# Second block's projection: value columns multiplied 512 at a time from a ring of four weight places, outputs stored by whole token tiles

## What is computed

```python
h = jnp.concatenate([meta, x], axis=1)             # 1040 x 1024
p = rms_norm_2(h, norm_mix_pre[l]) @ w_in[l]       # w_in: 1024 x 3080
pa = p[..., :A_COLS]                               # 512 columns, recurrent unit
pb = p[..., A_COLS:A_COLS + B_COLS]                # 512 q, 512 k, 512 v, 8 forget gates
pc = p[..., A_COLS + B_COLS:]                      # 1024 columns, delta rule
```

## Time and profile before

| | |
|---|---|
| median of 3 runs | 3685.35 us (3679.71 to 3690.36) |
| profiled execution, span first to last instruction | 3696.6 us |
| mean granted TensorE clock | 0.951 of full speed |
| PE busy | 3382.9 us, 92% of the span |
| DVE, ACT, POOL busy | 44%, 33%, 7% |
| DMA | 289.30 MB, mean 78 GB/s |
| the phase of the second projection | about 1825 to 2194.6 us of the span |
| its value part | 2099.1 to 2191.7 us |

### The profile page before, as it was taken

How to read it: one execution, slowest core, us unless ns; L and a number is a source line. 1 busy time by engine, 2 the same in 40 slices (tenths; PEclk the granted TensorE clock), 3 DMA queues, 4 the chain that set the end, 5 groups by cost and what they waited for, 6 DMA issues and landing times. The chain is left out here.

```text
span 3696.6 us, 52585 instructions
## 1 busy us (share of the span) xinstructions
PE 3382.9 (92%) x21754; PEld 2898.5 (78%) x21754; DVE 1628.7 (44%) x2517; ACT 1222.9 (33%) x2230; POOL 260.5 (7%) x332
## 2 busy tenths in 40 slices
PE   7899978999798999897999999887888899999998
PEld 2699976777587999775788985556666799999777
DVE  2306725666472111365444104554554455554343
ACT  3212315666562343125442103443322211111232
POOL 2000000000010000112201100001210000000010
PEclk9999998999899999998999996998999899999999
DMA  9224550000342221334211220001003111111332
GB/s 329 88 84 149 159 175 36 12 12 13 132 156 98 76 74 58 110 115 139 92 34 48 86 71 12 13 3 5 2 2 115 63 45 45 45 46 56 108 128 93
DMA packets 196721, 289.30 MB, mean 78 GB/s; under 512 B 41606, under 2 KB 137670, under 8 KB 194480
## 3 DMA queue, kind: packets, MB, share of 16 engines
q1 hardware_dynamic: 176624, 216.90, 18.0%
q0 software_dynamic: 19904, 69.65, 5.7%
HBM read 217.60 MB, written 68.90 MB: 78 GB/s over the span
## 5 line engine op out<-in xcount | busy, mean ns | idle before, releaser
L115 PE MATMUL p_pb<-p_w_hi,h_hi 128*128 128x416 f32 (+2 forms) x1216 | 425.1, 350 | 7.8 <-DVE p_w_lo L110 7.8
L117 PE MATMUL p_pb<-p_w_hi,h_lo 128*128 128x416 f32 (+2 forms) x1216 | 422.3, 347 | 0.0
L116 PE MATMUL p_pb<-p_w_lo,h_hi 128*128 128x416 f32 (+2 forms) x1216 | 420.0, 345 | 0.0
L115 PE MATMUL fu_pf<-h_hi,fu_w_hi 128*128 128x344 f32 (+1 forms) x1056 | 339.4, 321 | 8.6 <-DVE fu_pf L3439 8.6
L116 PE MATMUL fu_pf<-h_lo,fu_w_hi 128*128 128x344 f32 (+1 forms) x1056 | 340.3, 322 | 0.0
L117 PE MATMUL fu_pf<-h_hi,fu_w_lo 128*128 128x344 f32 (+1 forms) x1056 | 338.9, 321 | 0.0
L115 PEld LDWEIGHTS p_pb<-p_w_hi,h_hi 128*128 128x128 f32 x1216 | 229.4, 189 | 16.9 <-issue 15.5
L116 PEld LDWEIGHTS p_pb<-p_w_lo,h_hi 128*128 128x128 f32 x1216 | 229.5, 189 | 1.9
L117 PEld LDWEIGHTS p_pb<-p_w_hi,h_lo 128*128 128x128 f32 x1216 | 229.1, 188 | 0.7
L115 PEld LDWEIGHTS fu_pf<-h_hi,fu_w_hi 128*128 128x128 f32 x1056 | 199.9, 189 | 9.0 <-DVE fu_pf L3439 9.0
L117 PEld LDWEIGHTS fu_pf<-h_hi,fu_w_lo 128*128 128x128 f32 x1056 | 199.8, 189 | 0.0
(11 more groups left out here) (521 smaller groups left out, 7188.6 us busy)
## 6 DMA issues: line engine op xcount, KB each, us to landing
mod_w<-in_adaln_w SPq DMA_DIRECT2D x12, 2048.0 KB, 16.8
fu_raw<-in_ffn_up SPq DMA_DIRECT2D x88, 256.0 KB, 3.1
fd_raw<-in_ffn_down SPq DMA_DIRECT2D x44, 512.0 KB, 3.6
la_qkv<-p SPq DMA_DIRECT2D x16, 1024.0 KB, 4.9
p<-p_o SPq DMA_DIRECT2D x60, 208.0 KB, 1.9
s_raw<-in_w_in POOLq DMA_DIRECT2D x48, 256.0 KB, 3.5
rT<-p_stage SPq DMA_DIRECT2D x10, 896.0 KB, 4.8
p_raw<-in_ab_w_in POOLq DMA_DIRECT2D x10, 832.0 KB, 6.2
```

The costliest lines, as they stand in the source:

```text
L115: pe.matmul(out, left[0], right[0], start=start, stop=False)
L116: pe.matmul(out, left[0], right[1], start=False, stop=False)
L117: return pe.matmul(out, left[1], right[0], start=False, stop=stop)
```

## The change

A class `WeightRing` takes the place of `Weights` in this phase: one pair `w` of `[128, 8, 512]` with four places of 128 columns side by side; block `b` is made at place `b % 4`. The raw buffer is as before (one, in halves). The last four blocks, the value columns, fill all four places, and the value uses read 512 columns across them. A value use is now one token tile: 9 uses (21 to 29) of 24 matmuls with 512 moving columns, in place of 12 uses of 72 matmuls with 128. Since all value blocks must be in place before the first value use, the table `prepared_at` makes two blocks at the starts of blocks 17 and 18, one at 19, and the last one (23) at the start of use 21; that one overwrites block 19, which use 20 reads. The copy of a use is one of 128 x 512 (16 x 512 for the first) into the first 512 columns of the q/k output buffer `x`, and the store one of whole 2 KB rows. The buffers `vo` go.

```diff
...
+class WeightRing:
+    def __init__(self, ph, kd, blk, n):
+        self.half, self.blk, self.n = kd // 2, blk, n
+        self.raw = [ph.sb(f"raw{h}", [P, self.half, blk]) for h in range(2)]
+        self.w = ph.pair("w", [P, kd, n * blk])
+        self.raw_in = ph.sems("raw_in0 raw_in1")
+        self.hi_done = ph.sems("hi_done0 hi_done1")
+        self.lo_done = ph.sems("lo_done0 lo_done1")
+    def part(self, b, h, which):
+        c0 = self.blk * (b % self.n)
+        return self.w[which][:, self.half * h:self.half * h + self.half, c0:c0 + self.blk]
+    def load(self, eng, b, src):
+        for h in range(2):
+            if b:
+                eng.wait_ge(self.lo_done[h], b)
+            eng.dma_start(self.raw[h][:, :, :], src(self.half * h, self.half * h + self.half)).then_inc(self.raw_in[h], 16)
+    def make_hi(self, eng, b):
+        for h in range(2):
+            eng.wait_ge(self.raw_in[h], b * 16 + 16)
+            eng.activation(self.part(b, h, 0), self.raw[h][:, :, :], ACT.Copy).then_inc(self.hi_done[h], 1)
+    def make_lo(self, eng, b):
+        for h in range(2):
+            eng.wait_ge(self.hi_done[h], b + 1)
+            lo_part(eng, self.part(b, h, 1), self.raw[h][:, :, :], self.part(b, h, 0)).then_inc(self.lo_done[h], 1)
+    def ready(self, pe, b):
+        for h in range(2):
+            pe.wait_ge(self.lo_done[h], b + 1)
...
-    V_GROUPS = 3
-    n_uses = U_V + 4 * V_GROUPS
+    N_V = len(TILES2)
+    n_uses = U_V + N_V
+    RING = 4
+    B_V = NB - RING
-        w = Weights(ph, KD, P)
+        w = WeightRing(ph, KD, P, RING)
-        vo = [ph.sb(f"vo{b}", [P, 3, P]) for b in range(2)]
...
+        v_out = [x[:, b, 0:512] for b in range(2)]
...
             return t[:, 0:2 * CUT].rearrange("p (j t) -> p j t", j=2)
-        def v_tiles(m):
-            return [(3 * (m % V_GROUPS) + j, TILES2[3 * (m % V_GROUPS) + j]) for j in range(3)]
...
                     sp.dma_start(pT[P * m:P * m + P, :], qk_out[n % 2]).then_inc(qk_stored[n % 2], 16)
-                for m in range(4 * V_GROUPS):
+                for m in range(N_V):
                     n = U_V + m
-                    cols = slice(P * (m // V_GROUPS), P * (m // V_GROUPS) + P)
+                    t0, rr = TILES2[m]
                     sp.wait_ge(took[n % 2], n // 2 + 1)
-                    if m % V_GROUPS:
-                        t0 = TILES2[3 * (m % V_GROUPS)][0]
-                        sp.dma_start(pv[t0:t0 + 3 * P, cols].rearrange("(t p) d -> p t d", p=P), vo[n % 2][:, :, :]).then_inc(v_stored[n % 2], 16)
-                    else:
-                        sp.dma_start(pv[0:META, cols], vo[n % 2][0:META, 0, :]).then_inc(v_stored[n % 2], 16)
-                        sp.dma_start(pv[META:META + 2 * P, cols].rearrange("(t p) d -> p t d", p=P), vo[n % 2][:, 1:, :]).then_inc(v_stored[n % 2], 16)
+                    sp.dma_start(pv[t0:t0 + rr, :], v_out[n % 2][0:rr, :]).then_inc(v_stored[n % 2], 16)
                 sp.wait_ge(cum_out, 32)
...
                     sp.wait_ge(qk_stored[b], 16 * 4)
-                    sp.wait_ge(v_stored[b], 16 * 8)
-            def v_before(n):
-                return sum(1 if m % V_GROUPS else 2 for m in range(n - U_V) if (U_V + m) % 2 == n % 2)
+                    sp.wait_ge(v_stored[b], 16 * sum(1 for m in range(N_V) if (U_V + m) % 2 == b))
...
                 else:
-                    if v_before(n):
-                        eng.wait_ge(v_stored[b], 16 * v_before(n))
-                    if (n - U_V) % V_GROUPS:
-                        copy(vo[b][:, :, :], pb[b][:, :, 0:P]).then_inc(took[b], 1)
+                    m = n - U_V
+                    rr = TILES2[m][1]
+                    if m < 2:
+                        eng.wait_ge(qk_stored[b], 16 * 4)
                     else:
-                        copy(vo[b][0:META, 0, :], pb[b][0:META, 0, 0:P])
-                        copy(vo[b][:, 1:, :], pb[b][:, 1:, 0:P]).then_inc(took[b], 1)
+                        eng.wait_ge(v_stored[b], 16 * (m // 2))
+                    copy(v_out[b][0:rr, :], pb[b][0:rr, 0, :]).then_inc(took[b], 1)
...
                     return n
-                if n < U_V:
-                    return n - 1
-                return U_V - 1 + (n - U_V) // V_GROUPS
+                return min(n - 1, B_V)
...
-            def last_use_of(b):
-                return max(n for n in range(n_uses) if n != NARROW and block_of(n) == b)
+            def prepared_at(b):
+                if b < B_V - 3:
+                    return [b + 1]
+                return {B_V - 3: [B_V - 2, B_V - 1], B_V - 2: [B_V, B_V + 1], B_V - 1: [B_V + 2], B_V: [B_V + 3]}[b]
+            def use_of(b):
+                return b if b < NARROW else b + 1
...
                 turns = Turns(side())
-                w.make_hi(act, 0, 0)
+                w.make_hi(act, 0)
                 act.wait_ge(in_n, 16)
...
                 for n in range(n_uses):
-                    if starts_block(n) and block_of(n) + 1 < NB:
-                        b = block_of(n) + 1
-                        if b >= 2:
-                            m = last_use_of(b - 2)
-                            act.wait_ge(made[m % 2], m // 2 + 1)
-                        w.make_hi(act, b, b % 2)
+                    if starts_block(n):
+                        for b in prepared_at(block_of(n)):
+                            if b >= RING:
+                                m = use_of(b - RING)
+                                act.wait_ge(made[m % 2], m // 2 + 1)
+                            w.make_hi(act, b)
                     turns.to(3 * n + 1)
...
                 turns = Turns(side())
-                w.make_lo(dve, 0, 0)
+                w.make_lo(dve, 0)
                 dve.wait_ge(hi_n, 1)
...
                 for n in range(n_uses):
-                    if starts_block(n) and block_of(n) + 1 < NB:
-                        w.make_lo(dve, block_of(n) + 1, (block_of(n) + 1) % 2)
+                    if starts_block(n):
+                        for b in prepared_at(block_of(n)):
+                            w.make_lo(dve, b)
                     turns.to(3 * n + 2)
...
                     if starts_block(n):
-                        w.ready(pe, block_of(n))
+                        w.ready(pe, block_of(n) if n < U_V else NB - 1)
                     if n >= 2:
...
                     if n < U_V:
-                        s = block_of(n) % 2
-                        left = wn if n == NARROW else [h[:, :, :] for h in w.slots[s]]
+                        c_w = P * (block_of(n) % RING)
+                        left = wn if n == NARROW else [h[:, :, c_w:c_w + P] for h in w.w]
                         rows_ = FOX_HEADS if n == NARROW else P
...
                     else:
-                        s = block_of(n) % 2
-                        for j, (t, (c0, rr)) in enumerate(v_tiles(n - U_V)):
-                            for k in range(KD):
-                                mm = product(pe, pb[b][0:rr, j, 0:P], [h[:, k, c0:c0 + rr] for h in hT], w.cut(s, k, 0, P),
-                                             k == 0, k == KD - 1)
+                        c0, rr = TILES2[n - U_V]
+                        for k in range(KD):
+                            mm = product(pe, pb[b][0:rr, 0, :], [h[:, k, c0:c0 + rr] for h in hT], [h[:, k, :] for h in w.w],
+                                         k == 0, k == KD - 1)
                         mm.then_inc(made[b], 1)
...

...
```

## The result

Four executions of the changed kernel took 3646.26 to 3668.79 us, median **3649.49**, against 3679.71 to 3701.45, median 3687.86, of the kernel before: a ratio of 0.9902, 95% interval 0.9873 to 0.9931. Forecast were 3648.2 and 37.1 us less; the medians are 38.4 apart. The span of the profiled execution fell by more, from 3696.6 to 3649.3, that is 47.3 us.

A forecast was written before the change was run, and what follows sets the result against it. PE's matmul stream was taken to bound the kernel, its value part paced by 128-column stationary loads. Stream 91.5 to 49.1, ends +0.1, wait +3.2, clock +1.6, copy and store +0.4: -37.1 us from 3685.35, so 3648.2, range 3638 to 3659.

The forecast's parts named there:

- PE's stream: Value part: 216 matmuls of 512 columns at the rates of stages fd and xo, 49.1 us for 91.5.
- rival 3: Value matmuls: the 128-column load is not hidden behind 512 moving columns, 12 us more, so 3660 us; chance 0.02.
- rival 4: Value matmuls: only the load counts, as at 128 columns, 24.2 us for 49.1, so 3623 us; chance 0.01.
- The added wait: Ahead of the first value use: PE waits for block 23, made after use 20; +3.2 us, bounds 2.2 and 3.7.
- The clock behind it: After that wait: the idle time sends PE's clock to its lower level for a while; +1.6 us, ends 0 and 2.8.
- Rival 1's two halves: After the wait: the clock does not fall, or falls for longer; 3646.6 or 3649.4 us, chances 0.20 and 0.12.
- Two blocks at a time, copies, stores: Uses 18 and 19 and the value uses: extra blocks, copies and stores hidden, 0; last copy and store +0.4 us.
- The sum: Whole kernel: -91.5 + 49.1 + 0.1 + 3.2 + 1.6 + 0.4 = -37.1 us, giving 3648.2 us.
- the eight or so matmuls 0.427 us apart: Sign behind the idle stretch ahead of the first value use: some eight matmuls at the lower clock.
- weight loads busy half as much: Sign in the value part: PE's weight loads busy half as much, with 512-column matmuls about 0.227 us apart.
- every other phase as long as before: Sign outside the projection phase: all other phases keep their length, while this one ends about 37 us earlier.
- The range: Whole kernel's time: 3638 to 3659 us, leaving out rivals 3 and 4 and a part of the scatter.

The follow-up runs named there:

- both runs on width: split128 and split256: the changed kernel with each token tile multiplied in groups of 128 or 256 columns; projection phase 375.4 and 332.4 us.
- cover: Changed kernel with the first value use begun on the 384 columns already there, the last 128 after block 23; projection phase 328.4 us, execution 3659.4 us.
- after: First profiled execution of the changed kernel, against the kernel before; span 3649.3 us, projection phase 331.87 us, fx 289.4 us.
- again: The changed kernel profiled once more, unaltered; it repeated its projection phase and its fx (theory 331.9 us, rival 289.5 us).
- again5: Unaltered changed kernel against the kernel before, five rounds on another chip; ratio 0.9889, median 3648.95 us; profiled projection phase 335.1 us, fx 298.8 us.
- split256: Changed kernel with each token tile multiplied in two groups of 256 columns; projection phase 332.4 us, 0.1183 us per matmul.
- delay1: Changed kernel with one dependent DVE operation added ahead of the last value copy; fx 277.4 us.
- delay2_fill: The kernel of delay2 with 18 idle-filling identity matmuls added at the head of fx; fx 284.8 us.
- aligned: Changed kernel with token tiles cut at multiples of 128, so the stationary operand starts at multiples of 512 bytes; projection phase 334.0 us.
- delay2: Changed kernel with two dependent DVE operations added ahead of the last value copy; fx 298.8 us.
- split128: Changed kernel with each token tile multiplied in four groups of 128 columns, 864 matmuls again; projection phase 375.4 us.
- the five rounds: Unaltered changed kernel against the kernel before, on another chip; ratio 0.9889, interval 0.9866 to 0.9911, means 3654.4 and 3691.8 us.
- the fill: 18 more identity matmuls where PE waits at the head of fx, added to cover and delay2; fx 280.5 and 284.8 us.

## Why the prediction was right

- **PE's stream** (the term of 49.1 us for 91.5, right to 0.9). Measured 49.8 from first to last start, plus one distance 50.0. The rates taken from fd and xo were 0.227 and 0.232; the values' 128-row matmuls took 0.2316, 0.9 us more in all. The mechanism, a load of 128 stationary columns that sets the rate at 128 moving columns and is hidden at 512, is shown by both runs on width; rival 3 (load and columns add up) and rival 4 (the load alone counts) fell with them. The Trainium skill's 131 ns for 512 columns ("TensorE: Matmul & The Clock Gate", section "Back-to-back issue gap") does not hold here either: 231.6.
- **The added wait** (+3.2 us). PE restarted 2103.06 - 2099.66 = 3.40 us behind the last q/k matmul, where that distance was 0.15: +3.25. The idle stretch is 3.08, and cover shows that the wait goes when something stands in it.
- **The clock behind it** (+1.6 us). This is the term that was mis-sized. It is not one value: the clock stayed up in after, again, again5, split256, delay1 and delay2_fill and fell in aligned, delay2 and split128, each behind about 3.1 us of idle time. A fall costs 2.6 us (aligned), near the upper end of 2.8 that the earlier trace rows gave and not the earlier trace rows's 1.6. Rival 1's two halves are both real, and the forecast's middle was a case that no run showed at this place.
- **Two blocks at a time, copies, stores** (0, and +0.4 for the end). Hidden as said, with 3.4 us and more left ahead of the copies; PE never waited on a copy. From the last start to the next phase 2157.21 - 2152.86 = 4.35 us for 4.13: +0.2, and the matmul's own end is in it, for which +0.5 was set down.
- **The sum.** 50.0 for 91.5, +3.25 for the wait and +0.2 for the end give -38.0; the phases differ by -37.5 because the part ahead of the value uses lasted 0.57 longer in the profile after (from the phase's first matmul to the last q/k one 274.32 us for 273.75). That is not the change's: it arises ahead of the first product, which started 7.23 us into the phase for 6.66, and the same part took 273.8 to 274.3 in the other executions of both kernels' code in which no clock fell there. Against the forecast of -37.1 the terms are off by +0.9 (stream), -1.6 (clock), -0.3 (end) and +0.6 (head, not in the forecast), which cancel to -0.4. That the mechanism and the large terms are right is no luck; that the total is right to 0.4 us is. The means of the five rounds give -37.3. That the first two profiles differed by 47.3 would have misled anyone who read the gain off the spans.
- **Signs that did not come.** Three of those that the prediction named are not in the profile after: the eight or so matmuls 0.427 us apart (they stand in aligned and delay2), weight loads busy half as much (0.81 of the stretch), and every other phase as long as before (fx was 9.3 us shorter).
- **What I had not weighed:** that the spread of the executions comes mostly from one stage, fx, which took 276.2 to 298.9 us in eleven profiles at equal work (those with the fill left out), while all but fx and the projection phase took 3025.9 to 3034.3. The lengths are not spread evenly: five are 298.7 to 298.9, two 289.4, one 283.8 (aligned) and three 276.2 to 277.5. The range needed for this was there, as scatter, without its cause.

## What to carry to other kernels

When each matmul brings a new load of 128 stationary columns, look at the distance of starts: if it is that of the load (0.112 us here), widening the moving side is free up to the width where columns take over, here 256 of them. Judging by split256, four weight blocks side by side were not needed for it and two might do, with a smaller ring and less to wait for; that was not tried.

A wait that is new in a dense stream costs its length and, in three of nine executions here, a fall of the clock (2.6 us); let it fall where half of the operands are already good for something, as with the 384 columns of cover.

Compare a phase with the same phase, not a span with a span: a stage that isn't touched may add 20 us of either sign.

## What was not expected of the hardware

In fx PE was over 90% busy while the clock was at its lower level (25.86 of 27 us at 0.51 in delay2_fill), so a high busy share does not bring the clock back by itself there. Part of this share comes from the lower level itself: right behind, from 2204 to 2224 at 1.00, PE was busy for 16.47 of 20 us. fx's matmuls are over 66, 128 and 16 rows, most with 128 moving columns or fewer, with transposes and small waits between; which of this holds the clock down was not tested. Its length differed by 21 us between two kernels whose fx began 4 us apart and worked on the same data (delay1, 277.4; delay2, 298.8), and by 9.3 us between executions of one and the same kernel (after, again5). A matmul of 256 moving columns (0.118 us) took hardly longer than one of 128 (0.112) when each brought 128 stationary columns.
